# Values and seven heads' outputs transposed by VectorE and DRAM in the first layer of a two-layer hybrid decoder

## The reference, cut to what matters

```python
qkv, z, beta_logit, a_logit = split(x @ w_in)          # 3072 + 1024 + 8 + 8 columns
q, k, v = split(silu(causal_conv4(qkv)))               # per head 128 channels each
u = solve(I + lmat, v * beta)                           # chunked delta rule: per chunk a triangular solve
# per chunk n, in order, with a carried state of 128 x 128 per head:
v_new = u_n - w_n @ state;  o = q_n @ state + qk_n @ v_new;  state = decay * state + k_dec.T @ v_new
o = rmsnorm(o, norm_g) * silu(z)                        # norm_g: one weight per channel of a head, shared by heads
y = o @ w_out
```

## Time and profile before

| | |
|---|---|
| runs | 1043.11, 1043.57, 1043.82 us, median 1043.57 |
| profiled execution, span | 1042.2 us (the page gives no other time for it) |
| TensorE busy | 1020.4 us, 98% of the span |
| VectorE busy | 675.6 us, 65% |
| ScalarE busy | 500.7 us, 48% |
| GpSimd busy | 252.5 us, 24% |
| granted TensorE clock, mean | 0.998 |

### The profile page before, as it was taken

One profiled execution on the slowest core, in us unless ns is written; L12 is line 12 of the kernel. 1 busy time (PEld: TensorE's weight loads), 2 busy tenths in 40 slices (PEclk: granted clock), 3 DMA queues, 4 the chain that ended last, 5 costly groups with the idle time before them and its releaser, 6 DMA issues. The chain is left out here.

```text
span 1042.2 us, 17693 instructions
## 1 busy us (share of the span) xinstructions
PE 1020.4 (98%) x6286; PEld 835.3 (80%) x6286; DVE 675.6 (65%) x1575; ACT 500.7 (48%) x1397; POOL 252.5 (24%) x585
## 2 busy tenths in 40 slices
PE   7999999999999999999999999999999999999997
PEld 6888788888787888888888888888867777776885
DVE  4677667676757676744466566434367778789655
ACT  5556556666656575634462113212155665668000
POOL 1018483737382828371000000000100000000000
PEclk9999999999999999999999999999999999999999
DMA  6231403030303121213115212102000000013211
GB/s 207 63 86 42 97 25 94 23 95 23 96 21 79 39 76 42 57 44 92 40 42 172 70 61 78 55 9 63 21 15 27 22 21 22 21 62 101 101 41 60
DMA packets 84215, 62.64 MB, mean 60 GB/s; under 512 B 32128, under 2 KB 74272, under 8 KB 84128
## 3 DMA queue, kind: packets, MB, share of 16 engines
q1 hardware_dynamic: 49808, 44.68, 14.4%
q10 hardware_dynamic: 34320, 16.84, 6.3%
HBM read 55.18 MB, written 6.32 MB: 59 GB/s over the span
## 5 line engine op out<-in xcount | busy, mean ns | idle before, releaser
L708 PE MATMUL ps<-act_hi,w_hi 128*128 128x512 f32 x512 | 224.3, 438 | 0.8 <-DVE w_lo L1469 0.8
L708 PE MATMUL ps<-act_hi,w_lo 128*128 128x512 f32 x512 | 201.3, 393 | 0.0
L708 PE MATMUL ps<-act_lo,w_hi 128*128 128x512 f32 x512 | 200.2, 391 | 0.0
L1518 DVE SCALAR_TENSOR_TENSOR tok<-xs,convw,tok 128x512 f32<-128x512 f32 x144 | 114.4, 794 | 18.9 <-ACT xs L1211 17.1
L643 POOL TENSOR_TENSOR rank<-inverse,tok 128x60 f32<-128x60 f32 (+24 forms) x248 | 100.6, 406 | 93.6 <-DMA tok<-blocks_in 75.3
L708 PEld LDWEIGHTS ps<-act_hi,w_lo 128*128 128x128 f32 x512 | 96.1, 188 | 21.4
L708 PEld LDWEIGHTS ps<-act_hi,w_hi 128*128 128x128 f32 x512 | 97.0, 189 | 12.4 <-issue 1.1
L708 PEld LDWEIGHTS ps<-act_lo,w_hi 128*128 128x128 f32 x512 | 97.2, 190 | 9.8
L646 POOL TENSOR_TENSOR inverse<-inverse,rank 128x60 f32<-128x60 f32 (+24 forms) x248 | 95.1, 383 | 19.4
L906 PE MATMUL ps<-wo_hi,act_hi 128*128 128x512 f32 x224 | 88.4, 395 | 1.0 <-DVE wo_lo L1621 1.0
L906 PE MATMUL ps<-wo_lo,act_hi 128*128 128x512 f32 x224 | 87.6, 391 | 0.0
(11 more groups left out here) (272 smaller groups left out, 2244.4 us busy)
## 6 DMA issues: line engine op xcount, KB each, us to landing
w_raw<-in_a_w_in ACTq DMA_DIRECT2D x32, 512.0 KB, 4.2
tok<-in_x SPq DMA_DIRECT2D x8, 512.0 KB, 6.9
decay<-gc_rows SPq DMA_DIRECT2D x8, 512.0 KB, 5.0
tok<-blocks_in SPq DMA_DIRECT2D x32, 128.0 KB, 2.7
xres<-in_x SPq DMA_DIRECT2D x8, 512.0 KB, 3.5
ws_raw<-in_b_w_in SPq DMA_DIRECT2D x16, 256.0 KB, 2.6
z_raw<-in_b_w_in SPq DMA_DIRECT2D x8, 512.0 KB, 3.9
out<-yr SPq DMA_DIRECT2D x7, 512.0 KB, 2.6
```

The costliest lines, as they stand in the source:

```text
L708: mm = pe.matmul(ps[:, g % 2, :], lhs[:, k, :], rhs[:, k, HALF * b:HALF * (b + 1)], start=(i == 0), stop=(i == GROUP - 1))
L1518: ins = dve.scalar_tensor_tensor(conv[b], xs[:, b, k:k + HALF], convw[:, k, tile:tile + 1], conv[b], ALU.mult, ALU.add)
```

## The change

The eight value transposes on TensorE (TV) and seven of the eight output transposes (OT, all but the last head's) are gone, and with them ScalarE's copies out of PSUM. In their place VectorE issues one 32 x 32 block transpose of 128 x 1024 for each (kinds VT and OT in its order), which leaves every block in the wrong place among the partitions, and SyncE's queue writes the tile to DRAM and reads it back by four DMAs that put the blocks in place. `v_tok` and `tok` of layer 0 are laid out as (block, chunk, 32), so that those who read them use strided views. `norm_g` is multiplied into the output weights where they are split, and no longer in the gate's product. VT stands at place 1.2 without a shift by head, OT on VectorE at 3.285.

```diff
@@ tables
-          "TV": [1.268],                      # AT_PE; AT_ACT has "TV": [1.259]
-          "VS": [2.127]}
+          "VT": [1.2],
+          "OT": [3.285]}                      # AT_DVE
-TURN_KINDS = ("TK", "SC", "M", "AQ", "TV", "D")
+TURN_KINDS = ("TK", "SC", "M", "AQ", "D")
-                late = 0.0 if kind == "TQ" else ...
+                late = 0.0 if kind in ("TQ", "VT") else ...
@@ sync
+            def turn_values(h):
+                sp.wait_ge(s_vblock, h + 1)
+                if h >= 2:
+                    sp.wait_ge(s_vin, 64 * (h - 1))
+                sp.dma_start(v_turn[h % 2], v_tok[h % 2][:, :, :, :].rearrange("p b c i -> p (b c i)")).then_inc(s_vout, 16)
+                sp.wait_ge(s_vout, 16 * (h + 1))
+                for b in range(4):
+                    sp.dma_start(v_tok[h % 2][32 * b:32 * b + 32, :, :, :].rearrange("p a c i -> p a (c i)"),
+                                 v_turn[h % 2].rearrange("(a j) (b x) -> b j a x", a=4, b=4)[b]).then_inc(s_vin, 16)
+            def turn_output(h):
+                (the same with s_oblock, s_oout, s_oin, tok[:, h, :] and o_turn)
@@ sync, in the loop over heads, ahead of the wait for s_inv
                 if h + 1 < GH:
                     gc_broadcast(h + 1)
+                turn_values(h)
+                if h >= 2:
+                    turn_output(h - 2)
                 sp.wait_ge(s_inv, h + 1)
@@ sync, after the loop
+            turn_output(GH - 2)
@@ scale_values (gpsimd)
-                pool.wait_ge(s_tev, 2 * h + 2)
+                pool.wait_ge(s_vin, 64 * (h + 1))
@@ tensor
-            def turn_v(h): ...
-                pe.wait_ge(s_m, NT * min(h + 3, GH))      # transpose_out: its waits but s_oscaled
-                elif kind == "TV":
-                    turn_v(a)
-                elif kind == "OT":
+                elif kind == "OT" and a == GH - 1:
@@ scalar
-            def values(h): ...
-                act.activation(wo[i][0][k][:, :], out_raw[i][OUT_SLOT[i][k]], ACT.Copy)
+                act.activation(wo[i][0][k][:, :], out_raw[i][OUT_SLOT[i][k]], ACT.Copy,
+                               scale=norm_g[:, 0:1] if i == 0 else 1.0)
@@ vector
-                        dve.scalar_tensor_tensor(dst, zacc, norm_g[:, 0:1], dst, ALU.mult, ALU.mult)
+                        dve.tensor_tensor(dst, zacc.rearrange("p (c a i) -> p c a i", c=4, a=4), dst, ALU.mult)
+                elif kind == "OT" and h < GH - 1:
+                    dve.wait_ge(s_oscaled, h + 1)
+                    dve.transpose(tok[:, h, :].rearrange("p (b c i) -> p b c i", b=4, c=NT),
+                                  o_tok[:, :, :].rearrange("p c (b j) -> p b c j", b=4)).then_inc(s_oblock, 1)
+                elif kind == "VT":
+                    dve.wait_ge(s_silu, 6 * h + 6)
+                    if h >= 2:
+                        dve.wait_ge(s_av, NT * (h - 1))
+                    dve.transpose(v_tok[h % 2][:, :, :, :], vT[:, :].rearrange("p (c b j) -> p b c j", c=NT, b=4))\
+                       .then_inc(s_vblock, 1)
-                dve.tensor_tensor(wo[i][1][k][:, :], out_raw[...], wo[i][0][k][:, :].bitcast(F32), ALU.subtract)
+                    dve.scalar_tensor_tensor(wo[i][1][k][:, :], out_raw[...], norm_g[:, 0:1],      # layer 0
+                                             wo[i][0][k][:, :].bitcast(F32), ALU.mult, ALU.subtract)
...
```

More of the change, by code:

```diff
@@ L162, in plan @@
                     continue
-                late = 0.0 if kind == "TQ" else LATE_TURN[h] if kind in TURN_KINDS else LATE_SCAN[max(h, 0)]
+                late = 0.0 if kind in ("TQ", "VT") else LATE_TURN[h] if kind in TURN_KINDS else LATE_SCAN[max(h, 0)]
                 name, c = STEPS[i] if kind == "S" else (kind, i)
@@ L431, in hybrid_trunk @@
             L.append({n: sem(f"l{i}_{n}") for n in
[L432 to L435, removed]
+                      ("ohi", "olo", "wohi", "wolo", "y", "params", "yev", "st", "sqrt", "dve", "ln")})
+            if i == 0:
+                L[i].update({n: sem(f"l{i}_{n}") for n in ("xtr", "xhi", "xlo")})
+                L[i]["x"] = [sem(f"l{i}_x{j}") for j in range(2)]
+            else:
+                L[i]["o"] = [sem(f"l{i}_o{j}") for j in range(2)]
             L[i]["wr"] = [sem(f"l{i}_wr{j}") for j in range(max(OUT_SLOT[i]) + 1)]
@@ L503, in gc_broadcast @@
                 sp.dma_start(decay[:, :, :], gc_heads[h].partition_broadcast(P)).then_inc(s_gcb, 16)
+            def turn_values(h):
[8 more added lines that the diff above has]
+            def turn_output(h):
+                sp.wait_ge(s_oblock, h + 1)
+                if h >= 2:
+                    sp.wait_ge(s_oin, 64 * (h - 1))
+                sp.dma_start(o_turn[h % 2], tok[:, h, :]).then_inc(s_oout, 16)
+                sp.wait_ge(s_oout, 16 * (h + 1))
+                for b in range(4):
+                    sp.dma_start(tok[32 * b:32 * b + 32, h, :].rearrange("p (a x) -> p a x", a=4),
+                                 o_turn[h % 2].rearrange("(a j) (b x) -> b j a x", a=4, b=4)[b]).then_inc(s_oin, 16)
             gc_broadcast(0)
@@ L1244, in sums @@
                         act.activation(cut, cut, ACT.Square, accum_out=sc[out_sum][:, h, c:c + 1]).then_inc(done, 1)
-            def values(h):
-                for i in range(2):
-                    act.wait_ge(s_tv, 2 * h + i + 1)
-                    if h >= 2:
-                        act.wait_ge(s_av, NT * (h - 1))
-                    act.activation(v_tok[h % 2][:, 4 * i:4 * i + 4, :],
-                                   ps[:, 6 + i, :].rearrange("p (c q) -> p c q", c=4), ACT.Copy).then_inc(s_tev, 1)
             def squares(h, c):
@@ L1282, in high_wo @@
                     act.wait_ge(s_pv, UNITS)
-                act.activation(wo[i][0][k][:, :], out_raw[i][OUT_SLOT[i][k]], ACT.Copy).then_inc(L[i]["wohi"], 1)
+                act.activation(wo[i][0][k][:, :], out_raw[i][OUT_SLOT[i][k]], ACT.Copy,
+                               scale=norm_g[:, 0:1] if i == 0 else 1.0).then_inc(L[i]["wohi"], 1)
             for kind, a, b in ACT_PLAN:
@@ L1304, in _ @@
                     sums(h, (6, 7), "ssk", s_kd, s_sk)
-                elif kind == "TV":
-                    values(h)
                 elif kind == "R":
@@ L1609, in low_out @@
                 dve.wait_ge(L[i]["ohi"], k + 1)
[L1610 to L1611 removed]
+                if i == 0:
+                    dve.tensor_tensor(act_lo[:, k, :].rearrange("p (c a i) -> p c a i", c=NT, a=4),
+                                      tok[:, k, :].rearrange("p (a c i) -> p c a i", a=4, c=NT),
+                                      act_hi[:, k, :].bitcast(F32).rearrange("p (c a i) -> p c a i", c=NT, a=4), ALU.subtract)\
+                       .then_inc(L[i]["olo"], 1)
+                else:
+                    dve.tensor_tensor(act_lo[:, k, :], bT[:, k, :], act_hi[:, k, :].bitcast(F32), ALU.subtract)\
+                       .then_inc(L[i]["olo"], 1)
             def low_wo(i, k):
```

84 lines of the change are left out of this document (44 added, 40 removed), and 1 row of the table AT_ACT.

## The result

The changed kernel takes 1046.24 us, the median of 12 runs between 1042.68 and 1049.41. The kernel before took 1043.78 on the same chip, 12 runs between 1043.11 and 1044.18. The ratio is 1.002, with a 95% interval of 1.0012 to 1.0028: a little slower, where 1040.7 was forecast. The spread is a result too: before, the runs lie within 1.1 us, after, within 6.7. Two executions in the experiments' series that took two and five times the usual time, one of e13 (2036 us) and one of the kernel before beside it, are left out of all that follows.

The account below looks back on a forecast made before the run. TensorE was taken as the bound, by about a microsecond a head over VectorE's X. Of 15.5 us leaving it, the terms by head summed to 2.9 us gained: span 1042.2 to 1039.3, median 1043.57 to 1040.7, range 1035 to 1045.

Parts of the forecast that it names:

- new idle time of 8 to 13 us: TensorE, before lines 839 and 849: idle time of 8 to 13 us, released by VectorE's X and by the copies.
- Its wait and its output block are lost gain: 0: Level 0 of head 4: TensorE already waits 0.26 us for X, so removing the output block gains 0.
- Heads 2 to 4, 6 and the last: Level 2 gains 0.05, 0.2 and -0.6 us in heads 2 to 4; -0.2 in head 6, 0.88 in the last stretch.
- Heads 5 and 7: Head 5 gains 0.15 us at level 2; head 7 gains 0.65, as 1.2 of its gap goes to VT.
- Heads 0 and 1: Blocks stand well ahead of a group's end and the chain moves with TensorE: gain 0.88 us each.
- Head 6: VT after M3 finds no idle time ahead of X and costs 1.2 us; level 0 comes 0.2 later.
- The transpose was taken at 1.2 us: VectorE's transpose of 128 x 1024: 1.2 us, fifteen times, 18 us in all.
- rival C: Slower: the large transpose costs 1.76 us or waits for GpSimd; 1045.7 us, deciding from 1.52 us on; chance 0.14.
- GpSimd doesn't hold the transpose up: VectorE's single-input transpose doesn't wait for GpSimd; if it did, head 5 would lose 0.9 us more.
- rival D: Round trips make SyncE's queue late for the inverses, at 16 us each and not 9.5; 1050 us, chance 0.03.
- Rival B: VectorE's transposes are hidden and each head gains its gap, 9.0 us in all: 1034.6 us; chance 0.20.
- A: TensorE is the only bound and the whole 15.5 us come out: 1028 us; chance 0.08.

Follow-up runs that it names:

- e13: e9 with junk matmuls on TensorE ahead of the waits of levels 0 to 3; 1038.4 us, ratio 0.9949.
- e5: Changed kernel with junk matmuls of 128 x 512 filling TensorE's waits before level 0; 1041.51 us, ratio 0.9986.
- e14: Kernel before with 9 and 13 junk VectorE operations ahead of X in the stretches of heads 4 and 6; 1051.3 us, ratio 1.0076.
- e15: e14 with 8 and 9 junk matmuls on TensorE ahead of the waits for the late X; 1048.89 us, ratio 1.0049.
- e2: Changed kernel with VT moved to place 1.55, behind X, and OT to 3.37, behind the copies for level 2; 1039.33 us, ratio 0.996.
- e7: Changed kernel with only the values transposed by VectorE and DRAM, all outputs on TensorE again; 1041.83 us, ratio 0.9986.
- e3: e2 with X directly behind the last M of the next head; 1040.83 us, ratio 0.9985.
- e9: e3 with ScalarE's and VectorE's copies behind levels 0 and 1 placed earlier too; 1043.41 us, ratio 0.9997.
- e6: e2 with TensorE's waits before level 0 filled by junk matmuls; 1039.01 us, ratio 0.9954.

## Why the prediction was wrong

**The step that failed** is the price of the new waits. The prediction foresaw "new idle time of 8 to 13 us" before levels 0 and 2, and it came, 10.9 us. It priced that idle time at nothing but the gain not made (for head 4: "Its wait and its output block are lost gain: 0"), and the word clock doesn't stand in it: TensorE was taken to run as fast behind a wait as it did before. The runs show otherwise. The clock falls behind these waits, and the median of the changed kernel is at 0.992 where the kernel before is at 0.998: 6 thousandths of 0.97 us, 5.8 us of 1046.24, and without them 1040.4. Filled waits give 4.7 us of it back (e5), and two waits made by hand in the kernel before bring the loss there (e14, e15). No range was held open for it, and none of the rivals had it.

**The terms by head** can be read at level 2, where the stretches end (its start after less its start before, each less the one ahead of it). The last row is e5, whose trace has no fall:

| stretch of head | 0 and 1 | 2 | 3 | 4 | 5 | 6 | 7 | last | sum |
|---|---|---|---|---|---|---|---|---|---|
| predicted, us | -1.76 | -0.05 | -0.20 | +0.60 | -0.15 | +0.20 | -0.65 | -0.88 | -2.89 |
| after, us | -0.47 | -0.10 | -0.34 | +0.68 | -0.33 | +1.42 | -1.01 | -0.91 | -1.06 |
| e5, us | -0.51 | -0.16 | -0.31 | +0.40 | -0.55 | +0.24 | -1.03 | -0.92 | -2.84 |

- **Heads 2 to 4, 6 and the last**: within 0.2 us in e5. Heads 5 and 7 gained 0.4 us more than predicted each. That VT and OT fall where they do, and about what each delays, was right.
- **Heads 0 and 1** were mis-sized by 1.3 us. The blocks on TensorE were given their 0.88 each, and VectorE's transposes nothing. They cost 1.1 us there. With VT behind X (e2) X of head 1's stretch ends at 118.12, 1.51 us earlier than before (119.63); with VT ahead of it, as in after, at 119.18. VectorE, of the kernel before, of after (two rows) and of e2:

```profile
119.19 0.44 DVE L1669 STREAM_TRANSPOSE tok<-xT 32x256 f32<-32x256 f32 x1
```

```profile
109.04 1.23 DVE L1683 STREAM_TRANSPOSE v_tok<-vT 128x1024 f32<-128x1024 f32 x1
...
118.74 0.44 DVE L1705 STREAM_TRANSPOSE tok<-xT 32x256 f32<-32x256 f32 x1
```

```profile
117.68 0.44 DVE L1705 STREAM_TRANSPOSE tok<-xT 32x256 f32<-32x256 f32 x1
```

Some 0.3 us of it is head 0's VT (TensorE takes `kT` at 92.85 in after and at 92.57 in e2), the rest head 1's. e7, which has VT alone on VectorE, ends X at 119.24: it is VT and not OT. This also holds e7 back from its sum.
- **Head 6**: +1.42 in after and +0.24 in e5. The two falls put after 0.6 us behind e5 at level 2 of head 5's stretch and 1.8 us behind from head 6's on; the profiled runs differ by the same (1042.68 and 1040.86).
- **The sum is right in part by luck**: heads 0 and 1 are 1.25 us short, and the other stretches together gain 1.2 us more than predicted. So 1040.6 at equal clock beside a forecast of 1040.7 shows less than it seems to.

**Other points.** The transpose was taken at 1.2 us and took 1.23 to 1.25, so rival C (1.52 or more) was not it, though the sign was its. GpSimd doesn't hold the transpose up: at 326.12 it takes 1.23 us while GpSimd's scaling runs until 327.11, and the convolution behind it takes 0.70, about as predicted. That settles what no run showed then; the rule of the Trainium skill in "SBUF — State Buffer", Who interferes with whom, agrees in its second half too. The round trip takes 6.1 + 2.8 us and the issues between, and delays nothing: rival D is out. Rival B would have had X and the copies end where they did, at 1034.6. e2 makes that order, and reaches 1038.4 at equal clock; with X early too it is 1036.4 (e3). So the order was a part of what kept the gain away; what is left to B's 1034.6 and to A's 1028 no experiment has recovered.

**What stays open**: what decides in one execution whether the clock falls. In after's profiled run a wait of 2.14 us was followed by a fall and one of 2.52 us was not; a kernel's runs differ by 6.7 us. That falls come behind waits, and that filling the waits takes most of them away, is shown; a rule by which to foresee a single one, or how long it lasts, is not. Nor is shown why e13 stays 1.2 us above e9's line, or why heads 5 and 7 gained 0.4 us more than predicted.

## What to carry to other kernels

Work taken off the busiest engine isn't gained until its next wait has been shortened too, and on TensorE that wait has a second price: after idle times of 1 to 4 us beside small matmuls the clock fell to half for 3 to 17 us here in some executions and not in others. So price a new wait of TensorE at its length and at a possible fall besides (1.7 us for each 3.4 us at half clock, at most), read the granted clock in windows and over all runs before believing a median, and try first whether the work in front of the wait can go behind it in the other engine's order (here two numbers in a table, 6.9 us). Where a wait has to stay, matmuls into an unused bank kept the clock up in most runs, at 0.7 to 1.2 us of their own (e5, e6, e13 at equal clock).

## What the runs showed of the hardware that was not expected

- The same kernel's time went with its mean granted clock at 0.97 us for each 0.001, from 1042.68 us at 0.995 to 1049.41 at 0.989; in e15, with the waits filled, the runs lie within 0.5 us.
- A fall after one wait of 2.60 us lasted 17 us (e14), though TensorE was busy in every window behind the first; in after's profiled run two falls lasted 3.4 us each.
- Transposes of 128x128 and matmuls of 128x512 as filler gave the same mean clock, 0.9974 and 0.9973.
